# A hybrid layer stack: the order of work in the first mixer, the index scores, the attention and the delta-rule pairs

## The chip, the cores and the metric

One core of one Trainium2 chip runs the whole program, in 32-bit floats. The metric is device time in microseconds. The engines are TensorE (PE; PEld is its weight load), VectorE (DVE), ScalarE (ACT), GpSimd (POOL) and SyncE (SP). Each runs its own instructions in order, and they wait for each other by semaphores.

## The reference

Two blocks over a sequence of 512 tokens of width 1024.

```python
# block 1: x += gla_mixer(rms_norm(x)); x += sqrelu_mlp(rms_norm(x)); rms_norm(x)
q, k, v, r, gk_low = split(h @ w_in)          # 4 heads, keys 128, values 256 wide
log_a = log_sigmoid(gk_low @ w_gk_up + b_gk) / 16
# per chunk of 64 tokens, b = cumsum(log_a):
o_inter = (q * exp(b)) @ state
o_intra = tril(sum_k q_i k_j exp(b_i - b_j)) @ v
state = state * exp(b_last) + (k * exp(b_last - b)).T @ v
x += (rms_norm(o) * silu(r)) @ w_out          # r: the output gate

# block 2: x += merged @ w_out; x += sqrelu_mlp(rms_norm(x))
(g_qkv, g_z, g_a, g_b, a_q, a_k, a_v, i_q, i_k, i_w, gate_a, gate_b) = split(rms_norm(x) @ w_in)
qkv = silu(causal_short_conv(g_qkv, conv_w))  # 8 heads; q, k l2-normalized
o_gdn = rms_norm(gated_delta_rule_chunked(q, k, v, g, beta)) * silu(g_z)
a_q, a_k = rope(rms_norm(a_q)), rope(rms_norm(a_k))   # 8 query heads, 2 key heads
i_q, i_k = rope(i_q), rope(i_k)               # 8 index heads of 64
score = sum_h i_w[h] * relu(i_q[h] @ i_k.T)   # causal; the best 128 keys of a query
o_att = softmax over the chosen keys
merged = sigmoid(gate_a) * o_gdn + sigmoid(gate_b) * o_att
```

## The kernel before

Activations lie with the feature on the partition, 512 tokens along the free side. A weight of 1024 rows comes in **panels** of 128 columns (512 KB). A panel takes five steps, on two sets of buffers (raw, w_hi, w_lo, one bank in g_bank) in turn: SP loads it; ACT rounds it (`act_split`, w_hi); DVE (`dve_split`) or Pool (`pool_split`) makes the rest (w_lo); TensorE does 24 matmuls of 128x512, hi by hi, hi by lo and lo by hi for eight row blocks (`pe_panel`; `pe_part` is a quarter of it, `pe_eighth` an eighth); an engine takes the result out of the bank and signals bank_free. `Panel(base, per, h, u)` gives the number of panel u of head h; the order is written by hand in every engine's program, and no planner moves anything.

The stages follow each other: norm, first mixer (`pe_gla`, `act_gla`, `dve_gla`, and Pool's share), W_out and MLP of block 1, two norms, in1 of block 2 (`*_in1`: index queries and keys, attention keys, values and queries, output gates), attention (`*_att`), the delta-rule pairs (`*_gdn`), W_out and MLP of block 2.

**First mixer.** Each of the four heads has six panels: q, k, two of v, two of the output gate. The prologue runs all six of head 0. A body works on one head: products per level of the chunk recursion, transposes of v, sums, state, norm; between these steps TensorE does `part(...)`, quarters of the next head's six panels. The last body has no next head: its parts are eighths of the first two panels of W_out, behind a wait for gla_done at every part.

**in1.** 25 panels. Panels 0 to 8 run first; then the gates' transposes, five rotations (`pe_rope`: TensorE multiplies by a swap matrix, Pool multiplies by the cosine, DVE by the sine and adds, `rp_out`), norms of the two attention keys (`pe_rms`, `act_rms`, `dve_rms`), their rotations and the transposes of the two value heads. Behind these come the index scores: twelve steps, each two score products and two parts of panels 9 to 14, while DVE sums the scores. Pool masks the three query blocks (causal) between its splits of panels 10 to 16; then DVE finds the top-k (`MAX8`, L1331) and TensorE does the panels of the attention queries.

**Attention.** Eight heads in a loop, two ahead: per turn TensorE does scores(i+1), the transposes of the probabilities of head i, its values, and the rotation of the query of head i+2 (`turn`). ACT takes exponentials and sums, DVE scales queries (L1446), normalizes, finds the maximum of the scores, writes the output (L1454).

**Delta rule.** Four pairs of heads. A pair has ten panels (`gdn_panel(p, 0..9)`): six pass a convolution (`conv_in`, `silu`) whose inputs come through tanh tables on ACT, panels 6 to 9 are gates (`gate_z`, `gate_a`). Behind panel 8 (L1590 starts) come the products of the pair, then the inverse of a triangular matrix in levels (L1574, L2022), then the recursion over chunks. The lines that free a gate's bank, and ACT's order ahead of it:

```python
dve.scalar_tensor_tensor(zg[:, e], tz[u % 2], 1.0, g_bank[q.par][:], ALU.add, ALU.mult).then_inc(s["tz_d"], 1)
dve.wait_ge(s["tz_d"], i + 1)
dve.sem_inc(bank_free[q.par], 1)
```

## Time and profile before

| what | us |
|---|---|
| median of three runs | 1780.18 |
| lowest, highest | 1779.96, 1781.19 |
| the profiled execution | 1785.38 |
| its span in the trace | 1783.6 |
| first mixer's bodies | 80 to 261.56 |
| in1 | 685 to 870 |
| attention | 872.76 to 949 |
| delta-rule pairs | 949 to 1374 |

The span runs from the first to the last instruction of the profiled execution; that execution took 1.8 us more than its span. A timeline row gives the start of a group of instructions, its length, engine, line, operation, tiles, count, and in square brackets the engine's idle time before it with what ended it. An 'L' number is a line of the kernel.

### The profile page before, as it was taken

What the parts mean: (1) busy time and instruction counts of PE and PEld (TensorE: products, weight loads), DVE (VectorE), ACT (ScalarE), POOL (GpSimd) and SP (SyncE); (2) the same over time, 40 slices, a digit from 0 to 9 for tenths busy, and PEclk for the clock granted to TensorE, in tenths of its full rate; (3) what the DMA queues carried; (4) which work ended last, traced back from release to release, by engine and by line L of the source; (5) the groups of instructions that cost most, each with busy time, mean ns of one, the idle gap of its engine ahead of it and who ended that gap; (6) DMA issues with size and microseconds to landing.
All of it is one profiled execution on the core that took longest, in us unless ns stands there. A gap on an engine that the chain in (4) does not pass through costs nothing.

```text
span 1783.6 us, 24801 instructions
## 1 busy us (share of the span) xinstructions
PE 1659.3 (93%) x9418; PEld 1316.4 (74%) x9418; DVE 984.9 (55%) x1489; ACT 680.3 (38%) x1033; POOL 241.9 (14%) x220
## 2 busy tenths in 40 slices
PE   6899968999999987899879898998989899999999
PEld 4677757888888864567547786877878688888887
DVE  5455545444454455378775757566674544444453
ACT  6355543313132334223444535254443332313232
POOL 0134330000000030134210311304022000000000
PEclk7999979999999997899999999999999999999999
DMA  4222202333333332223102213121220233333333
GB/s 136 72 60 72 71 13 82 95 96 93 105 94 94 94 87 73 59 60 83 50 0 83 60 49 83 39 70 49 72 70 15 82 86 103 94 95 94 106 93 96
DMA packets 258157, 135.06 MB, mean 76 GB/s; under 512 B 10699, under 2 KB 254940, under 8 KB 258068
## 3 DMA queue, kind: packets, MB, share of 16 engines
q1 hardware_dynamic: 258068, 133.84, 26.6%
q8 instruction: 61, 1.00, 0.2%
q14 instruction: 28, 0.23, 0.0%
HBM read 131.64 MB, written 2.18 MB: 75 GB/s over the span
## 4 chain that ended last, share of the span: by engine, by line
PE 70%; DVE 11%; issue 10%; ACT 6%; POOL 3%; DMA 0%; DVEq 0%; POOLq 0%; PEldq 0%; ACTq 0%; SPq 0%; PEld 0%
PE bank L229 17%; PE bank L230 17%; PE bank L231 17%; PE bank L1574 3%; DVE arena L1880 3%; PE bank L491 2%; DVE w_lo L213 2%; ACT w_hi L209 2%; PE bank L493 1%; PE bank L492 1%; PE bank L1395 1%; PE bank L1416 1%; PE bank L1131 1%; PE bank L1590 1%; PE bank L1627 1%
## 5 line engine op out<-in xcount | busy, mean ns | idle before, releaser
L229 PE MATMUL bank<-h_hi,w_hi 128*128 128x512 f32 x984 | 401.7, 408 | 38.4 <-DVEq L1899 13.7
L230 PE MATMUL bank<-h_lo,w_hi 128*128 128x512 f32 x984 | 391.3, 398 | 0.0
L231 PE MATMUL bank<-h_hi,w_lo 128*128 128x512 f32 x984 | 390.9, 397 | 0.0
L213 DVE TENSOR_TENSOR w_lo<-raw,w_hi 128x1024 fp32r<-128x1024 f32 x218 | 281.2, 1290 | 141.3 <-ACT w_hi L209 139.4
L209 ACT CAST w_hi<-raw 128x1024 fp32r<-128x1024 f32 x234 | 245.1, 1047 | 254.5 <-PE bank L231 243.1
L229 PEld LDWEIGHTS bank<-h_hi,w_hi 128*128 128x128 f32 x984 | 189.8, 193 | 97.0 <-issue 36.7
L229 PE MATMUL bank<-m_hi,w_hi 128*128 128x512 f32 x608 | 238.7, 393 | 6.4 <-DVE w_lo L213 6.2
L231 PE MATMUL bank<-m_hi,w_lo 128*128 128x512 f32 x608 | 237.3, 390 | 0.0
L230 PE MATMUL bank<-m_lo,w_hi 128*128 128x512 f32 x608 | 237.2, 390 | 0.0
L230 PEld LDWEIGHTS bank<-h_lo,w_hi 128*128 128x128 f32 x984 | 190.6, 194 | 41.3 <-issue 3.2
L231 PEld LDWEIGHTS bank<-h_hi,w_lo 128*128 128x128 f32 x984 | 189.7, 193 | 41.0
L229 PEld LDWEIGHTS bank<-m_hi,w_hi 128*128 128x128 f32 x608 | 114.4, 188 | 33.2 <-issue 6.5
L231 PEld LDWEIGHTS bank<-m_hi,w_lo 128*128 128x128 f32 x608 | 114.5, 188 | 24.1
L230 PEld LDWEIGHTS bank<-m_lo,w_hi 128*128 128x128 f32 x608 | 114.6, 188 | 23.4
L948 DVE TENSOR_TENSOR arena<-bank,arena 128x512 f32<-128x512 f32 x64 | 44.3, 692 | 147.0 <-PE bank L231 147.0
L938 DVE TENSOR_TENSOR arena<-arena 128x512 f32<-128x512 f32 x64 | 44.3, 693 | 133.4 <-ACT arena L914 133.4
L491 PE MATMUL bank<-h_hi,w_hi 128*128 128x512 f32 x248 | 106.2, 428 | 0.0
L914 ACT ACTIVATE arena<-bank 128x512 f32<-128x512 f32 x64 | 38.3, 598 | 175.4 <-PE bank L231 175.4
L493 PE MATMUL bank<-h_hi,w_lo 128*128 128x512 f32 x248 | 97.2, 392 | 0.0
L492 PE MATMUL bank<-h_lo,w_hi 128*128 128x512 f32 x248 | 96.9, 391 | 0.0
L1574 PE MATMUL bank<-arena 64*64 64x64 f32 x1984 | 73.0, 220 | 7.1 <-DVE arena L2022 4.0
L1574 PEld LDWEIGHTS bank<-arena 64*64 64x64 f32 x1984 | 67.2, 134 | 13.2 <-issue 10.5
(273 smaller groups left out, 2027.9 us busy)
## 6 DMA issues: line engine op xcount, KB each, us to landing
raw<-in_l_w_ff SPq DMA_DIRECT2D x64, 512.0 KB, 4.0
raw<-in_w_in SPq DMA_DIRECT2D x64, 512.0 KB, 3.8
raw<-in_w_mlp_up SPq DMA_DIRECT2D x32, 512.0 KB, 4.0
raw<-in_w_mlp_down SPq DMA_DIRECT2D x32, 512.0 KB, 3.7
raw<-in_l_w_in SPq DMA_DIRECT2D x24, 512.0 KB, 3.8
raw<-in_l_w_out SPq DMA_DIRECT2D x8, 512.0 KB, 3.7
arena<-gb_rows SPq DMA_DIRECT2D x16, 256.0 KB, 4.6
raw<-in_w_out SPq DMA_DIRECT2D x8, 512.0 KB, 3.7
```

What stands on the lines that cost most here:

```text
L209: act.copy(w_hi[q.par][:], raw[q.par][:]).then_inc(s["w_hi_ready"], 1)
L213: dve.tensor_tensor(w_lo[q.par][:], raw[q.par][:], w_hi[q.par][:].bitcast(F32), ALU.subtract).then_inc(s["w_ready"], 1)
L229: pe.matmul(g_bank[q.par][:], w_hi[q.par][:, k], hi[:, k], start=(k == 0), stop=False)
L230: pe.matmul(g_bank[q.par][:], w_hi[q.par][:, k], lo[:, k], start=False, stop=False)
L231: last = pe.matmul(g_bank[q.par][:], w_lo[q.par][:, k], hi[:, k], start=False, stop=(k == KT - 1))
L491: pe.matmul(g_bank[q.par][:], w_hi[q.par][:, k], hi[:, k], start=(k == 0), stop=False)
L492: pe.matmul(g_bank[q.par][:], w_hi[q.par][:, k], lo[:, k], start=False, stop=False)
L493: last = pe.matmul(g_bank[q.par][:], w_lo[q.par][:, k], hi[:, k], start=False, stop=(k == KT - 1))
L938: dve.tensor_tensor(sq[:, u % 2], rl[:, u % 2], rl[:, u % 2], ALU.mult).then_inc(s["sqr"], 1)
L948: dve.tensor_tensor(down[:, u % 2], g_bank[q.par][:], r_sqr, ALU.mult).then_inc(s["dn"], 1)
L1574: return pe.matmul(o, left, right, start=True, stop=True, skip_group_check=True)
L1880: dve.scalar_tensor_tensor(y, ub[:, jj:jj + SEQ], w, y, ALU.mult, ALU.add).then_inc(s["c_chain"] if jj < CONV - 1 else s["c_y"], 1)
```

## The change

Four stages are reordered; no panel is computed differently.

- First mixer: the prologue runs four panels. A head's two output-gate panels are parts 0 to 7 of its own body, and parts 8 to 23 are q, k and both v of the next head. The first three parts stand ahead of v's transposes. The last body has the gate parts and then the eighths of W_out; its wait for gla_done stands once, at part 8. ACT and DVE split and evict in the new order; a tanh table is loaded in the prologue.
- in1: one index rotation each stands behind panels 2 to 4, one in the middle of panel 5, one behind it. The scores start behind panel 5, with panels 6 to 11 under them. The norms and rotations of the attention keys and the transposes of the values stand between score steps (`between`). Pool masks block 1 ahead of its first split, and block 2 and 3 between splits.
- Attention: unrolled. Scores run two heads ahead and `turn` three; r_sum has two sets.
- Delta rule: ACT's `decays` stands ahead of tanh(4), the four `l2_root` behind tanh(6), `to_end` behind tanh(7). `gate_z(p, 0)` stands ahead of silu(5), and the first gate frees its bank without waiting for its own signal. Pool's product for ek and the mask on dec move from ahead of the inverse to its levels 3 and 4, and `token_major` of kbe and ek change places.

```diff
         def pe_gla(pe):
-            for u in range(6):
+            for u in range(4):
...
+                        k = (j - 8) // 2
+                        if front or j < 8:
+                            pe_part(pe, Panel(N_GLA, 12, hp2, 6 * e + 4 + j // 4), j % 4)
+                        elif k < 2 * (GLA_H - 1):
+                            if j == 8:
+                                pe.wait_ge(s["gla_done"], GLA_H)
+                            pe_eighth(pe, Panel(N_WO0, 0, 0, j % 2), k, m_hi, m_lo)
...
+                part(0, 1, 2)
...
-                part(0, 1, 2)
...
+            for u in range(4):
                 q = Panel(N_GLA, 12, 0, u)
                 if u:
                     act_split(act, q.next())
-                if u < 2 or u >= 4:
+                if u < 2:
                     q_evac(0, 0, u, q)
+            tanh_tables(act)
...
-                decay(h, 3)
-                if front:
-                    q_evac(h + 1, e + 1, 0, q(0))
-                    act_split(act, q(2))
+                q_evac(h, e, 4, q(4))
+                act_split(act, q(6))
                 decay(h, 4)
                 decay(h, 5)
-                if front:
-                    q_evac(h + 1, e + 1, 1, q(1))
-                    act_split(act, q(3))
+                q_evac(h, e, 5, q(5))
+                act_split(act, q(7))
                 decay(h, 6)
                 decay(h, 7)
                 if front:
-                    act_split(act, q(4))
+                    q_evac(h + 1, e + 1, 0, q(6))
+                    act_split(act, q(8))
...
-                    act_split(act, q(6))
+                    q_evac(h + 1, e + 1, 1, q(7))
+                    act_split(act, q(9))
+                    act_split(act, q(10))
...
+                    if lv % 2 == 0 and (front or lv < 4):
+                        dve_split(dve, q(6 + lv // 2))
+                    if lv == 1 or lv == 3:
+                        evac(h, e, 4 + lv // 2, q(4 + lv // 2))
...
                 if front:
-                    evac(h + 1, e + 1, 4, q(4))
-                    dve_split(dve, q(6))
+                    evac(h + 1, e + 1, 2, q(8))
+                    dve_split(dve, q(10))
...
-            for u in range(9):
-                pe_panel(pe, Panel(N_IN1, 0, 0, u), h_hi, h_lo, s["h_ready"] if u == 0 else None, 2 * KT)
+            def index_rope(c):
+                if c == 0:
+                    pe.wait_ge(s["wk_sb"], 2)
+                    pe.wait_ge(s["t_in"], 16 * 7)
+                    pe.wait_ge(s["consts_in"], 64)
+                pe.wait_ge(s["in1"], c + 1)
+                pe_rope(pe, c, idx_ropes[c][1], swap_i)
+            for u in range(6):
+                if u == 5:
+                    for k in range(KT):
+                        pe_eighth(pe, Panel(N_IN1, 0, 0, u), k)
+                        if k == 3:
+                            index_rope(3)
+                else:
+                    pe_panel(pe, Panel(N_IN1, 0, 0, u), h_hi, h_lo, s["h_ready"] if u == 0 else None, 2 * KT)
                 if u == 1:
...
             for tt in range(TT):
                 last = pe.transpose(b[1][:, tt * 40:(tt + 1) * 40], gb[0:40, tt * P:(tt + 1) * P], ident[0:40, 0:40])
...
+            def between(step):
+                if step == 5:
+                    for i in range(2):
+                        pe.wait_ge(s["r_sq"], i + 1)
+                        if i == 1:
+                            pe.wait_ge(s["rp_ss"], 5)
+                        pe.matmul(b[4 + i][:], ones[:], key_r[i], start=True, stop=True).then_inc(s["r_ss"], 1)
+                if step in (8, 10):
+                    i = (step - 8) // 2
+                    pe.wait_ge(s["r_y"], 2)
+                    pe_rope(pe, 5 + i, ak[:, i], swap_a)
+                if step in (9, 10):
+                    i = step - 9
+                    pe.wait_ge(s["in1"], 8 + i)
+                    pe.wait_ge(s["r_y"], 2)
+                    if i:
+                        pe.wait_ge(s["av_sb"], i)
+                    for tt in range(TT):
+                        last = pe.transpose(b[4][:, tt * P:(tt + 1) * P], av[:, i, tt * P:(tt + 1) * P], ident[:])
...
             pe.wait_ge(s["rp_out"], 5)
+            pe.wait_ge(s["gbt_sb"], 1)
...
                     for c in range(2):
-                        pe_part(pe, Panel(N_IN1, 0, 0, 9 + i // 4), i % 4)
+                        pe_part(pe, Panel(N_IN1, 0, 0, 6 + i // 4), i % 4)
                         i += 1
-            for u in range(9 + i // 4, 9 + ATT_H):
...
+                act.activation(key_r[i], ak[:, i], ACT.Square).then_inc(s["r_sq"], 1)
+            for i in range(2):
+                act.wait_ge(s["r_ss"], i + 1)
+                act.activation(key_r[i], b[4 + i][:], ACT.Ln, scale=1.0 / P, bias=eps[:]).then_inc(s["r_ln"], 1)
+            for i in range(2):
+                act.wait_ge(s["r_ln"], i + 1)
+                act.activation(key_r[i], key_r[i], ACT.Exp, scale=-0.5).then_inc(s["r_r"], 1)
...
+                if h == 1:
+                    for i in range(2):
+                        act.wait_ge(s["av_ps"], i + 1)
+                        act.copy(v_key[i], tiles(b[4][:])).then_inc(s["av_sb"], 1)
...
+                if u == 5:
+                    for c in (3, 4):
+                        dve_rope(dve, c, idx_ropes[c][1], si)
...
+            def between(step):
+                if step in (1, 3):
+                    split(8 + step // 2)
+                if step == 6:
+                    for i in range(2):
+                        dve.wait_ge(s["r_r"], i + 1)
+                        dve.scalar_tensor_tensor(ak[:, i], ak[:, i], gains[:, G_KN:G_KN + 1], key_r[i],
+                                                 ALU.mult, ALU.mult).then_inc(s["r_y"], 1)
+                if step in (9, 10):
+                    dve_rope(dve, step - 4, ak[:, step - 9], sa)
...
+            def key_rope(i):
+                pool.wait_ge(s["r_y"], i + 1)
+                pool_rope(pool, 5 + i, ak[:, i], ca)
+            causal(1)
+            pool_split(pool, Panel(N_IN1, 0, 0, 10))
+            causal(2)
+            key_rope(0)
+            pool_split(pool, Panel(N_IN1, 0, 0, 11))
+            key_rope(1)
+            pool_split(pool, Panel(N_IN1, 0, 0, 12))
+            causal(3)
+            for u in range(13, 17):
+                pool_split(pool, Panel(N_IN1, 0, 0, u))
...
+            pe.wait_ge(s["nm_r"], TT)
+            scores(1, 1)
+            turn(2, 0)
+            for i in range(ATT_H):
+                e = i % 2
+                spread(i, e)
+                if i + 3 < ATT_H:
+                    turn(i + 3, 1 - e)
+                values(i, e)
+                if i + 2 < ATT_H:
+                    pe.wait_ge(s["nm_r"], TT * (i + 2))
+                    scores(i + 2, e)
...
+            exponentials(0, 0)
+            exponentials(1, 1)
+            for i in range(ATT_H):
                 for n, k in enumerate(K_ORDER):
                     act.wait_ge(s["pt_ps"], (TT - 1) * i + (1, 2, 3, 3)[n])
                     bk, o = t_at[k]
                     act.copy(p_t[:, koff[k]:koff[k] + SEQ - k * P], bk[:, o:o + SEQ - k * P]).then_inc(s["pt_sb"], 1)
...
+                if 0 < i < ATT_H - 1:
+                    exponentials(i + 1, 1 - i % 2)
...
             for i in range(ATT_H):
-                body(i // 2, i % 2, min(2, ATT_H - 1 - i))
+                if i + 3 < ATT_H:
+                    dve_rope(dve, i + 10, aq[:, (i + 1) % 2], sa)
+                output(i)
+                if i + 1 < ATT_H:
+                    normal(i + 1, (i + 1) % 2)
+                if i + 2 < ATT_H:
+                    scores(i + 2, i % 2)
+                if i + 4 < ATT_H:
+                    queries(i + 4)
...
-                        token_major(p, 1, [ek[:, 0], ek[:, 1]], s["ek_c"])
+                        token_major(p, 1, [kbe[:, 0], kbe[:, 1]], s["kbe_r"])
                     if lv == 3:
-                        token_major(p, 2, [kbe[:, 0], kbe[:, 1]], s["kbe_r"])
...
+                            pe.wait_ge(s["dec_r"], 2 * p + e + 1)
...
-                    act.wait_ge(s["tz_d"], i - 1)
+                    act.wait_ge(s["tz_d"], i if u == 7 else i - 1)
...
+                    if u == 4:
+                        decays(p)
...
-                    if u == 4:
-                        decays(p)
                 l2_logs(p)
-                l2_root(p, 0)
-                l2_root(p, 1)
                 act_split(act, gdn_panel(p, 8))
-                l2_root(p, 2)
-                l2_root(p, 3)
                 tanh(p, 5)
                 tanh(p, 6)
-                to_end(p)
+                for u in range(4):
+                    l2_root(p, u)
                 act_split(act, gdn_panel(p, 9))
                 tanh(p, 7)
+                to_end(p)
                 act_split(act, gdn_panel(p, 10))
...
-                dve.wait_ge(s["tz_d"], i + 1)
+                dve.wait_ge(s["tz_d"], i + e)
...
-                dve.wait_ge(s["dec_r"], 2 * p + e + 1)
+                dve.wait_ge(s["dm_c"], 2 * p + e + 1)
...
+                gate_z(p, 0)
                 silu(p, 5)
-                gate_z(p, 0)
...
-                for e in range(2):
-                    pool.wait_ge(s["dm_c"], 2 * p + e + 1)
-                    pool.tensor_tensor(dec[e], dec[e], mask(LEVELS + 1), ALU.mult).then_inc(s["dec_r"], 1)
-                for e in range(2):
-                    pool.wait_ge(s["ek_b"], 2 * p + e + 1)
-                    pool.wait_ge(s["l_y"], 4 * p + 2 * e + 1)
-                    pool.tensor_tensor(ek[:, e], ek[:, e], qkv[:, 3 * e + 1], ALU.mult).then_inc(s["ek_c"], 1)
...
+                    if lv == 3:
+                        for e in range(2):
+                            pool.wait_ge(s["ek_b"], 2 * p + e + 1)
+                            pool.wait_ge(s["l_y"], 4 * p + 2 * e + 1)
+                            pool.tensor_tensor(ek[:, e], ek[:, e], qkv[:, 3 * e + 1], ALU.mult).then_inc(s["ek_c"], 1)
+                    if lv == 4:
+                        for e in range(2):
+                            pool.wait_ge(s["qk_r"], 2 * p + e + 1)
+                            pool.tensor_tensor(dec[e], dec[e], mask(LEVELS + 1), ALU.mult).then_inc(s["dec_r"], 1)
```

## Rows read from the trace of the kernel before

**Rows 1.** The page: busy time of the engines, and the line of the clock.

```profile
PE 1659.3 (93%) x9418; PEld 1316.4 (74%) x9418; DVE 984.9 (55%) x1489; ACT 680.3 (38%) x1033; POOL 241.9 (14%) x220
...
PEclk7999979999999997899999999999999999999999
```

**Rows 2.** Timeline (start, us, engine line op, [idle before]): ACT, two panel splits, in1.

```profile
723.30 1.05 ACT L209 CAST w_hi<-raw 128x1024 fp32r<-128x1024 f32 x1 [0.17 <-ACT arena L1223]
...
728.74 1.05 ACT L209 CAST w_hi<-raw 128x1024 fp32r<-128x1024 f32 x1 [0.17 <-ACT arena L1223]
```

**Rows 3.** Timeline of TensorE: last front body and last body of the first mixer.

```profile
173.72 0.69 PE L506 MATMUL bank<-arena 128*64 128x64 f32 x16
...
220.53 0.69 PE L506 MATMUL bank<-arena 128*64 128x64 f32 x16
...
225.99 0.87 PE L506 MATMUL bank<-arena 128*64 128x64 f32 x16 [3.76 <-DVE m_lo L784]
...
261.56 0.79 PE L491 MATMUL bank<-m_hi,w_hi 128*128 128x512 f32 x1 [4.31 <-PEq L263]
```

**Rows 4.** Timeline of TensorE, between the projections of in1 and the scores.

```profile
738.76 0.44 PE L1170 MATMUL bank<-ident,arena 40*128 40x40 f32 x4
...
762.96 0.50 PE L491 MATMUL bank<-h_hi,w_hi 128*128 128x512 f32 x1
```

**Rows 5.** Timeline of DVE, attention.

```profile
898.38 0.69 DVE L1454 SCALAR_TENSOR_TENSOR arena<-arena,bank 128x512 f32<-128x512 f32 x1 [1.90 <-PE bank L1416]
...
900.72 0.17 DVE L1471 RECIPROCAL arena<-arena 128x4 f32<-128x4 f32 x1
...
904.21 0.75 DVE L1446 SCALAR_TENSOR_TENSOR arena<-q_all,gains,q_sq 128x512 f32<-128x512 f32 x1
...
906.86 0.69 DVE L1454 SCALAR_TENSOR_TENSOR arena<-arena,bank 128x512 f32<-128x512 f32 x1 [1.90 <-PE bank L1416]
```

**Rows 6.** Timeline of TensorE, attention.

```profile
904.39 2.43 PE L1416 MATMUL bank<-arena 128*128 128x512 f32 x8
906.65 1.02 PE L1131 MATMUL bank<-arena,swap_a 128*128 128x512 f32 x2
```

**Rows 7.** Waits (tile, line <- releaser: us, count, longest).

```profile
PE bank L229 <- DVEq L1899: 13.7, 4, 3.4
```

**Rows 8.** Timeline of TensorE: panel 8 of pair one, panels 7, 8 of pair two.

```profile
1001.60 0.77 PE L229 MATMUL bank<-h_hi,w_hi 128*128 128x512 f32 x1 [3.42 <-DVEq L1899]
...
1008.54 1.72 PE L1590 MATMUL bank<-arena 128*128 128x128 f32 x14
...
1098.72 0.50 PE L229 MATMUL bank<-h_hi,w_hi 128*128 128x512 f32 x1 [0.59 <-DVE w_lo L213]
...
1107.89 0.76 PE L229 MATMUL bank<-h_hi,w_hi 128*128 128x512 f32 x1 [3.43 <-DVEq L1899]
...
1116.20 3.73 PE L1590 MATMUL bank<-arena 128*128 128x128 f32 x32
```

**Rows 9.** Timeline of DVE, before the top-k and at the start of the attention.

```profile
812.82 1.48 DVE L1331 MAX8 arena<-arena 128x8 f32<-128x256 f32 x3 [4.67 <-POOL arena L1364]
...
872.76 0.75 DVE L1446 SCALAR_TENSOR_TENSOR arena<-q_all,gains,q_sq 128x512 f32<-128x512 f32 x1 [2.11 <-ACT q_sq L1274]
```

**Rows 10.** Timeline of ACT, second pair: decays, panel 5, tanh of panel 5.

```profile
1093.55 0.62 ACT L1773 ACTIVATE arena<-arena 128x512 f32<-128x512 f32 x1
...
1095.63 0.56 ACT L1734 COPY arena<-bank 128x512 f32<-128x512 f32 x1
...
1105.51 0.61 ACT L1750 ACTIVATE arena<-arena 128x512 f32<-128x512 f32 x1
```

**Rows 11.** Timeline of DVE, second pair: products of panel stage, level of the inverse.

```profile
1111.61 0.68 DVE L1932 TENSOR_TENSOR arena<-arena 128x512 f32<-128x512 f32 x1
...
1113.42 1.78 DVE L1932 TENSOR_TENSOR arena<-arena 128x512 f32<-128x512 f32 x1
...
1138.96 0.69 DVE L2022 TENSOR_TENSOR arena<-arena,bank 128x512 f32<-128x512 f32 x1 [1.84 <-PE bank L1574]
```

177 lines of the change are left out of this document (54 added, 123 removed).

## The prediction

> **What bounds the kernel now.** The page comes first: TensorE is busy for 1659.3 us of the 1783.6 us span, and its clock line (one digit for 44.6 us) falls below 9 in four slices only: the first, the sixth (the last body of the first mixer), and the sixteenth and seventeenth (the two norms and the rotations) [rows 1]. A TensorE-bound kernel is read by its holes. In the projections one panel follows the other in 728.74 - 723.30 = 5.44 us, which is 24 matmuls without a gap [rows 2]; this is the exchange rate for everything below, because the change touches no matmul of a panel. It moves work so that holes close. I then read TensorE's timeline where the work waits and found four holes, one for each part of the change: the last head of the first mixer [rows 3], the stretch of rotations between the last projection panel and the index scores [rows 4], the attention [rows 5, 6], and a stall ahead of panel 8 of each of the four delta-rule pairs [rows 7, 8].
>
> **Part A, first mixer.** Two panels (a head's output-gate panels) leave the prologue: 2 x 5.44 = 10.9 us less before the first body. Each front body still holds 24 quarter panels, the same matmul work, so its length stays 220.53 - 173.72 = 46.8 us [rows 3]: I take 0 for the three of them, with bounds of -1 and +2 each three together, because the split and eviction order on ACT and DVE shifts by one step and the copy of v's transposes now comes behind three quarter panels. The last body had 12 eighths of W_out (12 x 0.68 = 8.2 us; an eighth is 5.44/8) and took 261.56 - 220.53 = 41.0 us, though its own products are worth 46.8 - 6 x 5.44 = 14.2 us: some 18.6 us of it are waiting and slow clock, among it 3.76 us for m_lo of the head before, ahead of its first products, and 4.31 us at its end [rows 3]. The 10.9 us of gate panels go into that room. The wait for gla_done moves behind them, so the 3.76 us go; four eighths (2.7 us) now lie behind the last level, where nothing is waited for that they could cover, and the levels themselves end later by about what the gate parts exceed the old waits. I take +1.4 us for the body. The added tanh table load lies on ACT ahead of a wait for the panel. A = -10.9 + 1.4 = **-9.5 us** (-12 if the body even shrinks by 1 us, -5 if 40% of the panels' time doesn't find room).
>
> **Part B, rotations under panels.** Between 738.76 and 762.96 TensorE does the transposes of the gates, five index rotations, two key norms, two key rotations and the value transposes, each waiting for DVE or ACT: 24.2 us [rows 4]. This stretch goes. What comes back: the five index products, two key products and two ones-products, nine products of 512 columns; one of them is recorded as a pair of matmuls that takes 1.02 us [rows 6]; I take 1.0 each, 9.0 us. The gate transposes are 0.44 [rows 4], the value transposes twice that, 0.9. That is 10.3 us of work. New waits: scoring starts behind rp_out of rotation 4, whose DVE half is 900.72 - 898.38 less the 0.69 of the output, 1.65 us [rows 5]; about the same for the key norm's square behind panel 8 (1.6, bounds 0 and 3), and 0.6 for w_lo of panel 12, split by Pool late. Sum 24.2 - 10.3 - 3.9 = **-10.0 us** (range -7 to -14). The scores keep their pace: six panels lie under them as before, only three numbers earlier. The top-k can't turn this into nothing: before it, DVE waits 4.67 us for Pool's causal mask, queued behind a split [rows 9]; that mask is now ahead of splits 10 to 12 in part, and the three panels more that follow the scores put the end of TensorE's projections some 20 us behind the top-k. So TensorE sets the end of this stage, which the old 2.11 us wait of DVE for ACT's q_sq confirms from the other side [rows 9].
>
> **Part C, attention.** Now one head takes 906.86 - 898.38 = 8.48 us; TensorE waits in it and so does DVE (1.90 us before the output) [rows 5]. In the new order the loop closes over DVE: query scaling 0.75, TensorE's turn of it 1.02 [rows 6] (it stands ahead of the values), values to output 906.86 - 904.39 = 2.47 [rows 5, 6], output 0.69, normalizing and scores 904.21 - 900.72 = 3.49 [rows 5]: 8.42, less small overlaps, 8.35 us. The look-ahead thus takes the wait out but puts queries and turn in its place: -0.13 x 4 = -0.5 for the heads that still have a head four ahead. Heads 5 to 7 have neither: they run at TensorE's and DVE's remaining 6.4, so -4.2 for two of them and -1.5 for the last. The prologue now scales and rotates a third query and makes a second head's scores before the first output, 0.75 + 1.65 + 2.1 = 4.5 of DVE, in part in its idle time: +3.7. C = **-2.5 us** (0 to -6).
>
> **Part D, delta-rule pairs.** TensorE waits 13.7 us in four places, one in each pair, for a bank that DVE frees at L1899 [rows 7]. The chain behind it in the second pair: ACT's tanh(5) starts at 1105.51 [rows 10]; silu(5) and gate_z(0) follow on DVE, and TensorE starts panel 8 at 1107.89 after 3.43 us of waiting; panel 8 then takes 1116.20 - 1107.89 = 8.31 instead of 5.44 us, because the granted clock has fallen behind the stall: 2.87 us more; in the first pair the stall was the same 3.42 and the panel took 1008.54 - 1001.60 = 6.94, 1.50 more [rows 8]. Ahead of tanh(5) ACT does four decay exponentials, 1095.63 - 1093.55 = 2.08 us [rows 10], and four l2 roots of the same form. The change puts the first four ahead of tanh(4), where ACT was idle, and the roots behind tanh(6): tanh(5) comes 4.16 us earlier; and gate_z(0) now precedes silu(5) and frees its bank without waiting for its own predecessor's signal, 0.85 more. 5.0 us against a stall of 3.4: it goes, and with it the slow panel. The 0.59 us wait for w_lo ahead of panel 7 [rows 8] goes too, since ACT's split no longer queues behind the decays. The first pair gains 3.42 + 1.50 + 0.59 = 5.5, the others 3.43 + 2.87 + 0.59 = 6.9 (I count the third and fourth as the second, and so a little less, 6.8): 5.5 + 6.9 + 2 x 6.8 = **-26 us**. What is late next: w_lo of panel 8 and the bank, both within 1 us of panel 7's end (so a new wait of 0 to 1 us is inside the range, and a short one would keep part of the clock loss: that is rival 1); then the squares for the products, 1.4 us of margin. Pool's ek product and the dec mask move into the inverse's levels 3 and 4; there DVE waits for TensorE anyway (1.84 us at 1138.96 [rows 11]). Range -20 to -28.
> A row bears on that last move: beside a Pool product DVE's tensor-tensor takes 1.78 us, where the same one alone takes 0.68 [rows 11]. The Trainium skill (SBUF — State Buffer, Who interferes with whom) says that a DVE instruction with two SBUF inputs and a GpSimd one that reads SBUF lock each other out for a whole instruction; the trace agrees. By it the moved products could each hold up one DVE step of the inverse instead of one ahead of it.
>
> **Sum.** -9.5 - 10.0 - 2.5 - 26 = -48.0 us against the profiled execution of 1785.38 us: 1737.4. The profiled one is 5.2 us above the median of 1780.18, and the same difference taken from the median gives **1732 us**.
>
> **The rivals.**
> 1. The pair's stall stays in part: panel 8 waits 1 us or more for w_lo or its bank, and the clock falls as it does now. Then D loses half of its gain, -13, and the time is 1732 + 13 = 1745. For it: margins under 1 us. Against it: 5.0 us of lead for 3.4 of stall. Chance 0.12.
> 2. The attention becomes TensorE-bound, about 6.8 us a head (scores 2.26, spread 1.27, values 2.26, turn 1.02 [rows 6], the first two taken like the values), because the scaling overlaps more than I think: -1.6 x 5 = -8 more, 1724. Chance 0.07.
> 3. The Pool products collide with DVE steps that set the inverse's pace: +1.1 to 1.5 us a pair [rows 11], four pairs, 1737. Chance 0.03.
> 4. DVE becomes last in part B: the key norms and rotations, now on DVE between score steps, hold up the scores, and TensorE, in order, with them. Half of B's gain goes: 1737. Chance 0.03.
> 5. Slower: the clock. TensorE's matmuls take twice as long at 1.2 GHz as at 2.4, and panel 8 shows what a stall leaves behind: 2.87 us [rows 8]. If the shorter steps between the scores and the attention's new order held the granted clock at its lower level through both stretches, six panels would cost 5.44 x 0.88 = 4.8 more each and seven heads some 5 each: 29 + 35 = 64, and -48 + 64 = +16: 1796. It decides from some ten panels at the lower level (48/4.8). Against it: the clock digits of the old scores and attention are all 9 [rows 1]. The Trainium skill (TensorE: Matmul & The Clock Gate, HAM oscillation) tells of kernels whose recurring gaps keep the clock throttled; the trace doesn't show it for gaps as short as the attention's 1.9 us, where the digit stays 9. Chance 0.02.
>
> **How the numbers follow.** The forecast has 0.73. Range: the four parts' ends are -60 (all four good ends) and -32 (the bad end of D and half the way of the others), which gives **1720 to 1748**; rivals 1 to 4 are inside, rival 5 and some of the bad tail of D are not. A measurement of this kernel tells about 0.2%, 3.6 us, from no change; only rival 5, or three parts failing together, ends there or beyond: faster 0.97, same 0.01, slower 0.02.
>
> **What would show it.** Right: no wait of TensorE at L1899, tanh(5) some 4 us earlier against its panel, panel 8 in under 6 us; no 24 us stretch before the scores; prologue of four panels and a last body of 42 to 43 us; heads of 8.3 us in the attention, the last three near 6.5. Wrong: panel 8 behind a new releaser at the lower clock; a hole between score steps with DVE as releaser; front bodies above 47.5 us; a granted clock below 0.9 anywhere from the scores to the attention.

## The result, and the profile after

The changed kernel takes 1733.15 us (median of four runs, 1731.8 to 1734.77) against 1780.42 us before: 47.3 us less, a ratio of 0.9734 with a 95% interval of 0.9722 to 0.9745. The forecast was 1732. The profiled execution has a span of 1731.7 us, and its own time of 1733.44 us is at the median, while the profiled execution of before was 5 us above its median; the two traces therefore differ by 51.9 us and not by 47.3.

The page of the changed kernel, the lines that answer to [rows 1]:

```profile
PE 1636.1 (94%) x9418; PEld 1304.1 (75%) x9418; DVE 972.4 (56%) x1489; ACT 681.2 (39%) x1033; POOL 237.8 (14%) x220
...
PEclk8999989999999998999899999999999999999999
```

TensorE's busy share went from 93 to 94%. It is busy for 23 us less in all, although it does the same 9418 matmuls: fewer of them ran at the lower clock. The first, the sixth (the last body of the first mixer) and the sixteenth digit of the clock went from 7 to 8 and the seventeenth from 8 to 9; the twentieth (823 to 866 us, the seam ahead of the attention) is 8 where it was 9.

Both traces can be cut at the same places of TensorE's program (starts of instructions, us):

| stretch | before | after | difference |
|---|---|---|---|
| start to the first panel of W_out behind the mixer (A) | 261.56 | 251.66 | -9.90 |
| from there to the first panel of in1 | 416.42 | 416.44 | +0.02 |
| from there to the last query norm's product (B) | 191.91 | 178.56 | -13.35 |
| from there to the first panel of the pairs (C) | 79.09 | 76.76 | -2.33 |
| from there to the last transposes (D) | 830.76 | 804.39 | -26.37 |

**First mixer**, TensorE, timeline: the last body starts at 205.54, and W_out at 251.66 (to be read beside [rows 3]).

```profile
205.54 0.69 PE L506 MATMUL bank<-arena 128*64 128x64 f32 x16
...
227.44 0.77 PE L491 MATMUL bank<-m_hi,w_hi 128*128 128x512 f32 x1 [4.61 <-DVE arena L692]
...
251.66 0.79 PE L491 MATMUL bank<-m_hi,w_hi 128*128 128x512 f32 x1 [4.20 <-PEq L263]
```

The last body takes 251.66 - 205.54 = 46.12 us and has a new wait of 4.61 us, for DVE's product of the gate (L692), which frees the second bank.

**Rotations and scores**, TensorE: where [rows 4] had one stretch of 24.2 us, there are single rotations between panels, and three waits.

```profile
706.43 1.02 PE L1109 MATMUL bank<-arena,swap_i 128*128 128x512 f32 x2
...
706.88 0.79 PE L491 MATMUL bank<-h_hi,w_hi 128*128 128x512 f32 x1
...
716.34 0.70 PE L1198 MATMUL bank<-arena 64*128 64x256 f32 x4 [1.28 <-DVE arena L1123]
...
739.84 1.98 PE L1174 MATMUL bank<-arena,ones 128*128 128x512 f32 x4 [1.42 <-ACT arena L1247]
...
768.25 0.50 PE L229 MATMUL bank<-h_hi,w_hi 128*128 128x512 f32 x1 [0.15 <-POOL w_lo L219]
```

A rotation and the next matmul start 0.45 us apart, and that matmul takes 0.79 in place of 0.50; with both, each of the five rotations adds 0.9 us to the panels that it stands in or behind. The waits are 1.28 (ahead of the scores, for DVE's half of the last rotation), 1.42 (ahead of the key norms) and 0.15 us. DVE, beside [rows 9]:

```profile
770.69 1.48 DVE L1352 MAX8 arena<-arena 128x8 f32<-128x256 f32 x3 [0.56 <-POOL arena L1381]
...
849.53 0.75 DVE L1480 SCALAR_TENSOR_TENSOR arena<-q_all,gains,q_sq 128x512 f32<-128x512 f32 x1 [21.00 <-ACT q_sq L1281]
```

The first products behind that wait, TensorE:

```profile
850.34 2.08 PE L1109 MATMUL bank<-arena,swap_a 128*128 128x512 f32 x2 [2.55 <-DVE arena L1480]
...
854.06 4.63 PE L1419 MATMUL bank<-arena 128*128 128x512 f32 x8 [1.65 <-DVE arena L1123]
...
868.43 1.31 PE L1429 MATMUL bank<-ident,arena 128*128 128x128 f32 x10 [3.05 <-DVE arena L1507]
```

The wait for Pool's mask is 0.56 where it was 4.67 us, and DVE now stands still for 21.0 us between the top-k and the attention: TensorE's panels set the end of the stage, as forecast. The 2.55 us that TensorE waits for the first query were there before too.

**Attention**, beside [rows 5, 6], TensorE and then DVE:

```profile
877.44 1.12 PE L1109 MATMUL bank<-arena,swap_a 128*128 128x512 f32 x2 [1.19 <-DVE arena L1480]
...
908.20 2.40 PE L1438 MATMUL bank<-arena 128*128 128x512 f32 x8
...
914.20 2.40 PE L1438 MATMUL bank<-arena 128*128 128x512 f32 x8
```

```profile
872.80 0.69 DVE L1486 SCALAR_TENSOR_TENSOR arena<-arena,bank 128x512 f32<-128x512 f32 x1 [0.60 <-PE bank L1438]
...
880.76 0.69 DVE L1486 SCALAR_TENSOR_TENSOR arena<-arena,bank 128x512 f32<-128x512 f32 x1 [0.60 <-PE bank L1438]
...
904.64 0.69 DVE L1486 SCALAR_TENSOR_TENSOR arena<-arena,bank 128x512 f32<-128x512 f32 x1 [0.60 <-PE bank L1438]
```

One head takes 880.76 - 872.80 = 7.96 us, and TensorE waits 1.19 us of it for the query scaling (L1480); the last heads take 914.20 - 908.20 = 6.0.

**Pair 2**, beside [rows 8, 10, 11]: TensorE, ACT, DVE.

```profile
1071.77 0.47 PE L229 MATMUL bank<-h_hi,w_hi 128*128 128x512 f32 x1
...
1077.33 3.73 PE L1628 MATMUL bank<-arena 128*128 128x128 f32 x32
```

```profile
1069.62 0.63 ACT L1789 ACTIVATE arena<-arena 128x512 f32<-128x512 f32 x1
```

```profile
1058.87 2.33 DVE L1917 SCALAR_TENSOR_TENSOR arena<-arena,conv_w 128x512 f32<-128x512 f32 x3
...
1069.74 1.23 DVE L213 TENSOR_TENSOR w_lo<-raw,w_hi 128x1024 fp32r<-128x1024 f32 x1 [0.67 <-ACT w_hi L209]
1070.89 0.68 DVE L1934 SCALAR_TENSOR_TENSOR arena<-arena,bank 128x512 f32<-128x512 f32 x1
...
1075.26 0.69 DVE L1969 TENSOR_TENSOR arena<-arena 128x512 f32<-128x512 f32 x1
...
1077.06 0.68 DVE L1969 TENSOR_TENSOR arena<-arena 128x512 f32<-128x512 f32 x1
```

Panel 8 starts without a wait and takes 1077.33 - 1071.77 = 5.56 us. The group of waits for L1899 [rows 7] is gone in all four pairs.

### The profile page after: what moved, and what is told of

It reads as the page before. It is cut to its first block, busy times and chain, and to the rows that moved or that the text cites. A ratio compares the mean times of both kernels' runs of the same rounds, so it can differ in the third digit from the quotient of the medians.

```text
span 1731.7 us, 24741 instructions
## 1 busy us (share of the span) xinstructions
PE 1636.1 (94%) x9418; PEld 1304.1 (75%) x9418; DVE 972.4 (56%) x1489; ACT 681.2 (39%) x1033; POOL 237.8 (14%) x220
## 3 DMA queue, kind: packets, MB, share of 16 engines
q8 instruction: 62, 1.02, 0.2%
## 4 chain that ended last, share of the span: by engine, by line
PE 76%; DVE 11%; issue 7%; ACT 5%; POOL 1%; DMA 0%; DVEq 0%; POOLq 0%; ACTq 0%; SPq 0%; PEldq 0%
PE bank L229 18%; PE bank L230 18%; PE bank L231 18%; PE bank L1612 4%; PE bank L491 3%; PE bank L493 3%; PE bank L492 3%; DVE arena L1917 2%; DVE w_lo L213 2%; ACT w_hi L209 1%; PE bank L1438 1%; PE bank L1109 1%; PE bank L1628 1%; PE bank L1665 1%; PE bank L506 1%
## 5 line engine op out<-in xcount | busy, mean ns | idle before, releaser
L213 DVE TENSOR_TENSOR w_lo<-raw,w_hi 128x1024 fp32r<-128x1024 f32 x218 | 276.5, 1269 | 119.5 <-ACT w_hi L209 117.5
L229 PEld LDWEIGHTS bank<-h_hi,w_hi 128*128 128x128 f32 x960 | 182.5, 190 | 77.5 <-issue 22.8
L230 PEld LDWEIGHTS bank<-h_lo,w_hi 128*128 128x128 f32 x960 | 182.6, 190 | 40.1 <-issue 3.7
L231 PEld LDWEIGHTS bank<-h_hi,w_lo 128*128 128x128 f32 x960 | 182.3, 190 | 38.5
L2116 POOL TENSOR_TENSOR arena<-arena,half_masks 128x256 f32<-128x256 f32 x48 | 43.6, 931 | 313.2 <-DVE arena L1981 313.2
```

The costliest lines, as they stand in the source:

```text
L213: dve.tensor_tensor(w_lo[q.par][:], raw[q.par][:], w_hi[q.par][:].bitcast(F32), ALU.subtract).then_inc(s["w_ready"], 1)
L229: pe.matmul(g_bank[q.par][:], w_hi[q.par][:, k], hi[:, k], start=(k == 0), stop=False)
L230: pe.matmul(g_bank[q.par][:], w_hi[q.par][:, k], lo[:, k], start=False, stop=False)
L231: last = pe.matmul(g_bank[q.par][:], w_lo[q.par][:, k], hi[:, k], start=False, stop=(k == KT - 1))
L2116: pool.tensor_tensor(halves(a_lv[e][:, lv % 2]), a_tr[e], half_mask(lv + 1), ALU.mult).then_inc(s["al_r"], 1)
```

## The experiments

In each run the edit is made in the changed kernel, unless it says otherwise. Ratios are against runs of the kernel before on the same chip; the changed kernel itself, run once more, gave 1733.24 us and 0.9729 (0.9713 to 0.9745).

> The changed kernel itself, once more, beside the next three on one chip: 1733 us again within 2 us. In the traces so far the same code reaches W_out between 249.85 and 252.46 us, by when the granted clock comes back after the first waits; theory 1 says that this is chance from run to run, so that this run's trace falls between or near them; theory 2 says that it hangs on the kernel, and then 251.66 comes again.

The new trace had 251.88 us for W_out, 0.2 us from the first one, which is what theory 2 named; and it lies between the others, which is what theory 1 named. So this run doesn't decide between them. What differs between the traces is the clock early in the program. The same matmuls of the same code, in the trace of undo_b and in that of the changed kernel:

```profile
55.16 0.40 PE L229 MATMUL bank<-h_hi,w_hi 128*128 128x512 f32 x1
```

```profile
55.71 0.63 PE L229 MATMUL bank<-h_hi,w_hi 128*128 128x512 f32 x1
```

Both stand behind a wait for w_lo that ended at 53.7 us (2.77 and 3.51 us long). In undo_b the clock stays at its full level, 0.40 us a matmul; in the changed kernel it falls at 54.9 us, to 0.63 us a matmul, and is back at 58.2. In twelve traces whose code is the same up to the last body of the first mixer, the first head's body began between 64.80 and 67.79 us, and the ten of them that also have the same last body reached W_out between 249.85 and 253.22 us. Whether that is chance from execution to execution, or hangs on something in each kernel, stays open; for the first speaks that the four executions of one kernel, c_queries_first, took 1724.76 to 1730.31 us. In either case a stretch of one trace that contains such a place can't be read more finely than some 2 us.

### The four parts, each undone alone

undo_a, undo_b, undo_c and undo_d take the lines of one part back to the kernel before, as the diff above shows them; the four together are the whole change.

> The changed kernel with part A undone alone (first mixer as before). Theory 1, the parts stand apart, and each is worth what its stretch of the two traces differs by: W_out's start came 9.90 us earlier, so this run is 9.9 us slower than the changed kernel (about 1743.0 us against 1733.15). Theory 2, part of that gain is in the clock's state that one stage hands to the next: 7 us or less.

> The changed kernel with part B undone alone (rotations back in one stretch between the panels and the scores). Theory 1: 13.3 us slower than the changed kernel (1746.5 us), as the stretch from panel 2 of in1 to the first query of the attention shortened from 176.6 to 163.3 us. Theory 2: the profiled execution of before was 5.2 us above its median, and this excess lies in the rotation stretch with its fallen clock; then B is worth what the prediction said or less, 8 to 10 us (1741 to 1743).

> The changed kernel with part C undone alone (attention two ahead, in loops). Theory 1: 2.3 us slower than the changed kernel (1735.5 us), the attention back from 73.9 to 76.2 us. Theory 2, the later start of the first output and the earlier end cancel and the difference is the clock's: within 1 us.

> The changed kernel with part D undone alone (order of the pair's tanh, roots, decays and gates, and Pool's products as before). Theory 1: the four waits of 3.4 us at the bank of panel 8 come back with the slow panel behind each, 5.8 us for the first pair and 7.1 for each other: 27 us slower than the changed kernel (1760 us). Theory 2, Pool's products inside the inverse cost something now and the order on ACT brings more than the total: still 27 us here, but parted otherwise when the halves are run alone.

| part undone | median us | ratio to before (95%) | part's worth by ratios | by its stretch, before against after | by its stretch, this run against after |
|---|---|---|---|---|---|
| A | 1740.42 | 0.9789 (0.977 to 0.9808) | 9.8 | 9.9 | 7.2 |
| B | 1743.17 | 0.9796 (0.978 to 0.9812) | 11.0 | 13.3 | 11.8 |
| C | 1735.54 | 0.9752 (0.9736 to 0.9769) | 3.2 | 2.3 | 3.7 |
| D | 1757.01 | 0.9868 (0.9851 to 0.9884) | 23.9 | 26.4 | 23.9 |

The worth by ratios is the difference from 0.9734 times 1780 us; with the intervals of both it holds to about 4 us for one part, and for the sum to about 10. The four add to 47.9 us, the whole gain is 47.3: nothing speaks against theory 1, that the parts stand apart, but the runs could not show an interplay of a few us. By medians alone A is worth 7.3 us and the sum is 43.5; the intervals don't tell these apart, nor the two theories of undo_a. The clock's place above enters A's last column: the trace of undo_a reached W_out at 258.81 us with the clock up at 55 us, and undo_b, with the clock up there too, at 249.85; like for like A is worth 9.0 us. For B the last column lies between the two theories: 1.6 us of the 13.3 (191.91 against 190.34 us) belonged to the profiled execution of before. The attention's stretch behind it was 75.52 us in undo_b and 76.76 in the changed kernel, but 75.26 in undo_a, where B and C are as changed: this 1.2 us is not B's.

The stall comes back in undo_d with the length it had before, and the price of the clock behind it differs from pair to pair. TensorE, panel 8 and the products of pairs 1 and 2:

```profile
976.55 0.47 PE L229 MATMUL bank<-h_hi,w_hi 128*128 128x512 f32 x1 [3.41 <-DVEq L1937]
...
983.73 3.73 PE L1628 MATMUL bank<-arena 128*128 128x128 f32 x32
...
1081.48 0.47 PE L229 MATMUL bank<-h_hi,w_hi 128*128 128x512 f32 x1 [3.39 <-DVEq L1937]
...
1087.04 3.86 PE L1628 MATMUL bank<-arena 128*128 128x128 f32 x32
```

After 3.41 us of waiting panel 8 took 7.18, after 3.39 us it took 5.56, which is the full clock; pairs 3 and 4 took 8.11. The whole D stretch was 828.27 here against 830.76 us before, so 2.5 of D's 26.4 us were the profiled execution's of before, and the run came out 3 us below the 27 of theory 1.

### Part D taken apart

d_act_order (ACT):

```diff
-                if u == 4:
-                    decays(p)
                 if u < 5:
                     tanh(p, u)
+                if u == 4:
+                    decays(p)
             l2_logs(p)
+            l2_root(p, 0)
+            l2_root(p, 1)
             act_split(act, gdn_panel(p, 8))
+            l2_root(p, 2)
+            l2_root(p, 3)
             tanh(p, 5)
             tanh(p, 6)
-            for u in range(4):
-                l2_root(p, u)
+            to_end(p)
             act_split(act, gdn_panel(p, 9))
             tanh(p, 7)
-            to_end(p)
```

> The changed kernel with only ACT's order of the pair undone (decays behind tanh(4), roots ahead of tanh(5)); DVE's gate order and Pool's places stay new. Theory 1, the leads add up in time: tanh(5) falls back by 4.16 us, gate_z(0) keeps its 0.85, so the stall ahead of panel 8 is 3.4 - 0.85 = 2.6 us in each pair, with the fallen clock behind it in most: 4 x 2.6 + 7 + 4 x 0.6 (panel 7's w_lo) = about 19 us slower than the changed kernel (1752 us). Theory 2, a stall of 2.6 us is short enough to leave the clock alone: 12 to 13 us (1746 us).

1752.28 us, ratio 0.9842 (0.9814 to 0.987): 19 us slower, as theory 1 said, but not by its sum. The wait ahead of panel 8 is 3.04 us, not 2.6:

```profile
1078.21 0.47 PE L229 MATMUL bank<-h_hi,w_hi 128*128 128x512 f32 x1 [3.04 <-DVEq L1938]
```

```profile
1077.32 0.69 DVE L1936 SCALAR_TENSOR_TENSOR arena<-arena,bank 128x512 f32<-128x512 f32 x1 [0.82 <-ACT arena L1789]
```

DVE itself waits 0.82 us for ACT there: with the old order of ACT, gate_z(0) stands behind tanh(6), and going ahead of silu(5) brings it only 0.4 us. The clock fell behind two of the four waits: panel 8 took 7.18, 5.53, 5.57 and 6.99 us after 3.04 to 3.07 us of waiting. Over the D stretch TensorE stood idle for 14.7 us more than in the changed kernel and was busy for 7.7 us more with the same matmuls. The four executions lie far apart (1749.26 to 1758.43 us), and the interval of the ratio allows 14 to 24 us.

d_dve_order:

```diff
-                    act.wait_ge(s["tz_d"], i if u == 7 else i - 1)
+                    act.wait_ge(s["tz_d"], i - 1)
...
-                dve.wait_ge(s["tz_d"], i + e)
+                dve.wait_ge(s["tz_d"], i + 1)
...
-                gate_z(p, 0)
                 silu(p, 5)
+                gate_z(p, 0)
```

> The changed kernel with only DVE's order of silu(5) and gate_z(0) and the wait on the gate's own signal undone. In the changed kernel's trace gate_z(0) ends at 1071.57 and panel 8 starts at 1071.77. Theory 1: that margin of 0.2 us is less than the 0.85 us that the old order costs, so each pair waits about 0.65 us: 2.6 us slower (1735.8 us), clock untouched. Theory 2: even so short a wait costs the clock: 2.6 + 7 = about 10 us. Theory 3: ACT's order alone was enough: no difference.

1734.95 us, ratio 0.9749 (0.9733 to 0.9765). Each pair has this wait, and panel 8 runs at the full clock behind it:

```profile
1070.16 0.47 PE L229 MATMUL bank<-h_hi,w_hi 128*128 128x512 f32 x1 [0.76 <-DVEq L1936]
```

Four times 0.76 is 3.0 us; the D stretch is 2.2 us longer than the changed kernel's. Theory 1 fits: these short waits cost their own length, and theory 2's 10 us are outside the interval. The median's 1.8 us is within its uncertainty. The margin of 0.2 us that the theories start from was none: here too 0.2 us pass between the end of gate_z(0), at 1069.96, and the start of TensorE, at 1070.16, which had been waiting for it.

d_pool_place (Pool's ek product and dec mask back ahead of the inverse, with the transposes' order that goes with it):

```diff
+                for e in range(2):
+                    pool.wait_ge(s["dm_c"], 2 * p + e + 1)
+                    pool.tensor_tensor(dec[e], dec[e], mask(LEVELS + 1), ALU.mult).then_inc(s["dec_r"], 1)
+                for e in range(2):
+                    pool.wait_ge(s["ek_b"], 2 * p + e + 1)
+                    pool.wait_ge(s["l_y"], 4 * p + 2 * e + 1)
+                    pool.tensor_tensor(ek[:, e], ek[:, e], qkv[:, 3 * e + 1], ALU.mult).then_inc(s["ek_c"], 1)
                 for lv in range(LEVELS):
```

> The changed kernel with only Pool's products and the order of kbe and ek undone (ek's product and dec's mask ahead of the inverse). Theory 1: the inverse starts 9.12 us behind the products in both traces, so Pool's place is worth nothing: within 1 us of the changed kernel. Theory 2: with the products now reached earlier against Pool, its 5 us ahead of the levels are late and hold the inverse back: 1 to 1.5 us a pair, 4 to 6 us slower.

1743.77 us, ratio 0.9795 (0.9779 to 0.9812): 10.6 us slower. Neither theory had the size, and the place is another than theory 2 said. Pool, DVE and TensorE of pair 2:

```profile
1057.67 2.72 POOL L2119 TENSOR_TENSOR arena<-arena,masks 128x512 f32<-128x512 f32 x2 [55.24 <-ACT arena L1811]
```

```profile
1057.70 1.54 DVE L1913 TENSOR_SCALAR arena<-arena,conv_w 128x512 f32<-128x512 f32 x1
1059.28 3.24 DVE L1916 SCALAR_TENSOR_TENSOR arena<-arena,conv_w 128x512 f32<-128x512 f32 x3
```

```profile
1076.15 1.67 POOL L2123 TENSOR_TENSOR arena<-arena 128x512 f32<-128x512 f32 x1 [15.76 <-ACT arena L1817]
```

```profile
1076.59 1.79 DVE L1968 TENSOR_TENSOR arena<-arena 128x512 f32<-128x512 f32 x1
...
1079.50 1.75 DVE L1968 TENSOR_TENSOR arena<-arena 128x512 f32<-128x512 f32 x1
```

```profile
1073.10 0.47 PE L229 MATMUL bank<-h_hi,w_hi 128*128 128x512 f32 x1 [1.11 <-DVEq L1935]
...
1081.31 2.05 PE L1628 MATMUL bank<-arena 128*128 128x128 f32 x16 [0.73 <-DVE arena L1968]
```

Dec's mask now runs at 1057.67 beside DVE's convolution, three steps of which take 3.24 us; in the changed kernel they take 2.33. The convolution's first step, which multiplies by one number per partition, takes 1.54 us where it takes 0.48. That makes tanh(4), the next split and tanh(5) late, and panel 8 waits 1.11 us. Ek's product at 1076.15 runs beside the product of the keys and beta (L1968), which takes 1.79 and 1.75 us where it takes 0.68 in the changed kernel, and the products wait 0.73 us. Together with 0.47 us for panel 7's w_lo these are 2.3 us in pair 2, and 1.9 in each of the others, where the products wait 0.38: 8.1 us. The D stretch is 12.2 us longer: TensorE is idle in it for 9.3 us more, and busy for 2.9 us more with the same matmuls, which is the clock's part. The mechanism is the one of [rows 11] for the steps with two operands in SBUF, beside a Pool product. That agrees with the Trainium skill (SBUF — State Buffer, Who interferes with whom). Moving the products into the inverse also lengthens a DVE step there, L1944 at 1092.44, which takes 1.66 us where the pair's other one takes 0.68, but ahead of a wait of 1.40 us for TensorE:

```profile
1092.44 1.66 DVE L1944 SCALAR_TENSOR_TENSOR arena<-arena 128x512 f32<-128x512 f32 x1
...
1095.50 0.69 DVE L2059 TENSOR_TENSOR arena<-arena,bank 128x512 f32<-128x512 f32 x1 [1.40 <-PE bank L1612]
```

### First mixer: what holds the last body

a_panel0_first:

```diff
-                        k = (j - 8) // 2
+                        k = (j - 8) % 6
...
-                        elif k < 2 * (GLA_H - 1):
+                        elif j < 20:
...
-                            pe_eighth(pe, Panel(N_WO0, 0, 0, j % 2), k, m_hi, m_lo)
+                            pe_eighth(pe, Panel(N_WO0, 0, 0, (j - 8) // 6), k, m_hi, m_lo)
```

> The changed kernel with one edit: in the last body the six eighths of W_out's panel 0 come first and those of panel 1 behind them, in place of turn and turn about. In the changed kernel TensorE waits 4.61 us at 227.44 for the gate's product on DVE (it frees the second bank), and the clock falls behind it. Theory 1: that wait is for panel 1's bank alone, and with panel 0's eighths ahead it goes with the slow stretch: 4 to 6 us faster (1728 us). Theory 2: the levels' own chain on DVE and ACT is as late as the bank, and the wait moves to the next products: within 1 us.

1733.62 us, ratio 0.9733 (0.9717 to 0.9749): no difference that can be measured, theory 2. The last body takes 251.19 - 206.42 = 44.8 us in place of 46.1. The 4.61 us wait is gone, and in its place the level's products wait for Pool, with the clock down behind them:

```profile
230.15 1.12 PE L506 MATMUL bank<-arena 128*64 128x64 f32 x16 [2.64 <-POOL arena L816]
```

DVE's exponent for that level queues behind its split of W_out's second panel, so ACT and Pool are late with the level; and that split itself starts at 224.47, after 2.45 us of waiting for ACT's w_hi.

### Versions that go further

c_queries_first:

```diff
-                if i + 2 < ATT_H:
-                    scores(i + 2, i % 2)
                 if i + 4 < ATT_H:
+                    dve.wait_ge(s["s_ps"], (TT - 1) * (i + 3))
                     queries(i + 4)
+                if i + 2 < ATT_H:
+                    scores(i + 2, i % 2)
```

> The changed kernel with one edit in the attention: DVE scales the query of the head four ahead before it reads the scores, behind a wait for TensorE's scores, and not behind them. Theory 1, the loop closes over the query scaling and the turn, as the prediction said: the period falls from 7.96 by the 1.19 us that TensorE waits for L1480 in each of four turns, to about 6.8 us: 4 to 5 us faster (1728.5 us). Theory 2, DVE's own work or the exponentials set the period: the wait moves to the output or the normalizing and the period falls by 0.5 us or less, 0 to 2 us.

1725.83 us, ratio 0.9688 (0.9672 to 0.9704): 7.4 us faster than the changed kernel by medians. DVE's outputs:

```profile
880.76 0.69 DVE L1486 SCALAR_TENSOR_TENSOR arena<-arena,bank 128x512 f32<-128x512 f32 x1 [0.36 <-PE bank L1438]
...
887.28 0.69 DVE L1486 SCALAR_TENSOR_TENSOR arena<-arena,bank 128x512 f32<-128x512 f32 x1 [0.36 <-PE bank L1438]
```

The period is 6.52 us and TensorE has no wait left in it. The loop did close over the query scaling (theory 1). Four periods give 4 x 1.44 = 5.8 us; the stretch is 5.6 us shorter, and the 7.4 us of the medians agree with that within their uncertainty of about 3 us.

q_exps_early:

```diff
                     act.activation(q_sq[:, h - 1], b[4 + h % 2][:], ACT.Ln, scale=1.0 / P, bias=eps[:]).then_inc(s["r_ln"], 1)
-            for h in range(ATT_H):
-                act.wait_ge(s["r_ln"], h + 3)
-                act.activation(q_sq[:, h], q_sq[:, h], ACT.Exp, scale=-0.5).then_inc(s["r_r"], 1)
+                    act.wait_ge(s["r_ln"], h + 2)
+                    act.activation(q_sq[:, h - 1], q_sq[:, h - 1], ACT.Exp, scale=-0.5).then_inc(s["r_r"], 1)
...
+            pe.wait_ge(s["r_ln"], ATT_H + 1)
             turn(0, 0)
```

> The changed kernel with one edit at the end of in1: ACT takes the exponential of each query norm behind its logarithm and not all eight at the end, and the first turn waits for the logarithm of head 6 (its bank). In the changed kernel DVE stands still for 21.0 us until the first exponential at 848.41, and TensorE waits 2.55 us for the first query. Theory 1: the first query is long ready, so that TensorE's turn starts at its last norm product's end: 3 to 4 us faster (1729.5 us), more if the clock now stays up through the turn. Theory 2: the exponentials delay ACT's splits and banks under the panels: no gain or a loss.

1727.3 us, ratio 0.9696 (0.968 to 0.9713): 5.9 us faster, more than the wait. TensorE at the seam:

```profile
846.73 1.13 PE L1214 MATMUL bank<-q_sq,ones 128*128 128x512 f32 x2 [0.56 <-ACT q_sq L1275]
...
847.69 1.02 PE L1109 MATMUL bank<-arena,swap_a 128*128 128x512 f32 x2
...
850.36 2.43 PE L1418 MATMUL bank<-arena 128*128 128x512 f32 x8 [1.65 <-DVE arena L1123]
```

The turn starts at once. And it takes 1.02 and the first scores 2.43 us, where the changed kernel, after its wait of 2.55 us, had 2.08 and 4.63 us at the lower clock: the stretch is 6.8 us shorter, 2.6 of waiting and about 4 of clock.

combined: the edits of c_queries_first, q_exps_early and a_panel0_first, and

```diff
-                    if lv % 2 == 0 and (front or lv < 4):
+                    if lv == 0 or (front and lv % 2 == 0):
                         dve_split(dve, q(6 + lv // 2))
                     if lv == 1 or lv == 3:
                         evac(h, e, 4 + lv // 2, q(4 + lv // 2))
+                    if lv == 3 and not front:
+                        dve_split(dve, q(7))
```

> The two edits above together, with panel 0's eighths first in the last body of the first mixer and DVE's split of W_out's panel 1 behind the gate's product, so that the exponents of the levels no longer queue behind it. Theory 1, they add: 4.5 + 3.5 + 2 to 3 = 10 to 11 us faster than the changed kernel (1722.5 us). Theory 2, what the attention gains at its start it loses against its own loop, and the last body's levels stay on Pool's and ACT's chain: 6 us (1727 us).

1717.96 us, ratio 0.9635 (0.9612 to 0.9658): 15.3 us faster than the changed kernel, more than either theory said. The stretch of C is 64.16 us, 12.6 less; the last body takes 41.6 us (206.29 to 247.88), 4.5 less, as the waits in it shrink:

```profile
228.93 0.69 PE L506 MATMUL bank<-arena 128*64 128x64 f32 x16 [1.11 <-POOL arena L818]
...
247.88 0.79 PE L491 MATMUL bank<-m_hi,w_hi 128*128 128x512 f32 x1 [4.20 <-DVEq L263]
```

In the C stretch the two edits add (5.6 + 6.8 = 12.4 us). The order of the split and the gate's product was not run by itself; against a_panel0_first it took another 3.2 us from the last body. This is the fastest version that was run.

## Why the prediction was right, point by point

The direction and the size were right, 1732 against 1733.15, and so was the bound: holes of TensorE closed. The parts came out at 9.8, 11.0, 3.2 and 23.9 us by ratios, against 9.5, 10.0, 2.5 and 26. That they came so close is in part luck: inside A, B and C terms were off and cancelled.

**A.** The prologue gave 78.45 - 66.48 = 12.0 us in the traces, 1.1 more than two panels. The first body lost 2.4 us (from 48.46 to 46.10): before, it waited 2.34 us for ACT ahead of its transposes, which I hadn't counted. The front bodies are 46.5 us against 46.8. What was wrong is "so the 3.76 us go" with +1.4 for the last body: it grew by 5.1 us (41.03 to 46.12), because another wait, of 4.61 us, took the place of that one behind the gate panels, with the clock down behind it. The a_panel0_first and combined runs show the chain: DVE's split of W_out's second panel and the exponent behind it. The sum held because the prologue and the first body gave 3.5 us that were not in it.

**B.** New work and waits were put at 14.2 us. By the rows it is 4.4 for five rotations, 1.7 for the gates' transposes with their wait, 3.3 for the norms with theirs, 1.8 for the key rotations, 1.0 for the value transposes and 0.15: 12.4. That leaves 24.2 - 12.4 = 11.8; the rest of the 13.35 us is in part w_lo waits under panels 2 to 8 (2.52 us before, 1.66 now), and 1.6 us were that execution's, as undo_b's 11.8 says.

**C.** The loop closed as forecast, at 7.96 us against 8.35: the recorded lengths of DVE's steps from the output to the next scaling were added (4.18 us), but each begins a little ahead of its predecessor's recorded end (3.84 us). The first output came 872.80 - 849.53 = 23.3 us after the first query, 6.1 us later than before (889.91 - 872.76 = 17.15), where I had 3.7:

```profile
889.91 0.69 DVE L1454 SCALAR_TENSOR_TENSOR arena<-arena,bank 128x512 f32<-128x512 f32 x1 [1.56 <-PE bank L1416]
```

The first scores ran at the lower clock in both kernels; the turns around them did so for 1.4 us more in the changed one. The other 4.7 us lie between the second head's scores and the first values: a third turn and a wait of 3.05 us for DVE's normalizing (L1507), which now stands behind a second head's scores and a third rotation. Outputs 4 to 7 took 18.0 against 24.4 us, 6.4 us where I had 5.7, and the four periods before them gave 2.1 us where I had 0.5. So +6.1 - 2.1 - 6.4 = -2.4 meets the -2.5 by three errors that cancel.

**D.** The stall, the slow panel and panel 7's wait went, as forecast. Mis-sized was the clock's price: I took it at 1.5 to 2.9 us in each pair, and undo_d shows that it can be nothing in one. And "Pool's ek product and the dec mask move ... there DVE waits anyway" was costed at nothing, which holds for where they went, but not for where they left: with ACT's decays earlier they would have met the convolution and the keys' product, at 10.6 us. The stretch is a gain only as a whole; what I called the lead, 5.0 us, needed Pool out of the way. The lead itself was over-counted too. Tanh(5) came 4.2 us earlier against the start of panel 6, as forecast (12.98 us behind it before, 8.81 after). But the 0.85 us of gate_z(0) shrank to 0.2: in the changed kernel it starts when DVE's split of w_lo ends (1069.74 and 1.23 us), 1.3 us behind the start of tanh(5). And panel 8 is due 0.6 us sooner, since panel 7 no longer waits. And the starts behind the two old waits had made panels 6 and 7 longer by 0.5 us. Nothing was left of the margin of 1.6 us: panel 8's first matmul comes 0.08 us late in pair 2.

**Rivals.** Number 1 didn't come, though no margin was left; and d_dve_order and d_pool_place show that its price was too high, since waits of 0.76 and 1.11 us left panel 8 at the full clock. Number 2 didn't come: at 7.96 us a head TensorE still waited 1.19 us; the c_queries_first run brought it, by another order. Number 3 names the contention that d_pool_place shows, though there it is with the convolution and the keys' product and not in the inverse. Number 4 didn't come: the only wait between score steps is 1.42 us, for ACT. Number 5, the clock, appeared only in the seam behind the query norms, where the granted clock of slice 20 is 0.88, one of the signs named for "wrong"; before, the same seam had it too (0.92 in its slice). The 1.9 us that the rival calls the attention's gap is DVE's wait; TensorE's there was 1.65 us.

## What to carry to other kernels

Where one engine is the bound, count its holes with their releasers and ask of each what in the releaser's own queue stands ahead without need: four exponentials and four roots ahead of the tanh that frees a bank cost 19 us here, one scaling behind a read 6, eight exponentials kept for the end 6. When a step is made earlier, look at what else is released by it: here Pool's products would have run earlier too and into DVE's two-operand steps. And where a wait is covered by new work, the next one on the same chain can take its place.

## What the hardware showed

- The same 3.4 us wait of TensorE ahead of the same panel left the clock at the full level once and at the lower level three times in undo_d (panel 8 in 5.56 against 7.18 and 8.11 us); 3.04 to 3.07 us did each twice in d_act_order. Waits of 0.76 and 1.11 us left it up.
- In all twelve traces with the wait of 2.55 us ahead of the first turn of the attention the first scores ran at the lower level, most of them in 4.63 us; in the two without it, q_exps_early and combined, they ran at the full one, in 2.43 us.
- With the same code ahead of it, the moment at which the first head's body began moved by up to 3 us from trace to trace (64.80 to 67.79 us), with the clock; whether by chance or by kernel stays open.
- Beside a Pool product a DVE product of 512 columns took 1.75 to 1.79 us for 0.68, three convolution steps 3.24 for 2.33, and a product by one number per partition 1.54 for 0.48.
